# Another tile order in the second dilated attention stage, and the turned blocks beside one step

## The reference

```python
oa, _ = banded_attention(qa, ka, va, WINDOW_A, S, sink)    # 8 heads of 64, keys within 128 tokens
oa = rms_norm(oa.reshape(n, S, D_A), g_oa)
ob = dilated_mixture(qb, kb, vb)                           # 8 heads of 64, each key of the stream by its mask
ob = rms_norm(ob.reshape(n, S, D_B), g_ob)
return jnp.concatenate([oa, ob], axis=-1) @ w_out
```

## Time and profile before

| what | value |
|---|---|
| median of three runs | 2294.83 us (2293.78 to 2295.69) |
| profiled execution: time, span | 2295.82 us, 2294.0 us |
| mean granted TensorE clock | 0.984 |
| TensorE busy | 2194.8 us (96%) |
| VectorE, ScalarE, GpSimd busy | 49%, 28%, 34% |

### The profile page before, as it was taken

The page is one execution under the profiler, slowest core; times in us unless marked ns, Lnnn a source line. Parts: engine busy times, 40 slices in busy tenths (PEclk is TensorE's granted clock), DMA queues, the critical chain, the costliest instruction groups (busy, mean ns, idle before and its releaser), DMA issues. The chain is left out here.

```text
span 2294.0 us, 35862 instructions
## 1 busy us (share of the span) xinstructions
PE 2194.8 (96%) x13528; PEld 1928.1 (84%) x13528; DVE 1134.4 (49%) x2157; ACT 631.9 (28%) x1562; POOL 787.3 (34%) x442
## 2 busy tenths in 40 slices
PE   7999989999999999999998999999999999999997
PEld 7889877888888888888898888789878888888885
DVE  3575655536555145325355766454465532542353
ACT  3445454234311011001044454443242110110002
POOL 3311202441344444444331111034323444444443
PEclk9999989999999999999999999799999999999998
DMA  6200021321122211222241000122111122222222
GB/s 214 71 19 29 29 74 36 93 74 34 51 65 64 64 62 58 64 64 64 65 147 38 29 29 28 65 83 67 62 38 56 57 63 64 64 64 64 64 64 84
DMA packets 41988, 144.86 MB, mean 63 GB/s; under 512 B 4880, under 2 KB 5136, under 8 KB 41616
## 3 DMA queue, kind: packets, MB, share of 16 engines
q1 hardware_dynamic: 34560, 119.02, 16.7%
q10 hardware_dynamic: 7312, 24.21, 3.0%
HBM read 133.78 MB, written 9.44 MB: 62 GB/s over the span
## 5 line engine op out<-in xcount | busy, mean ns | idle before, releaser
L751 POOL CAST w_hi<-w_landed_tile 128x1024 fp32r<-128x1024 f32 x216 | 225.1, 1042 | 1468.7 <-PE ps L798 1456.6
L798 PE MATMUL ps<-x_turned,w_hi 128*128 128x512 f32 (+1 forms) x3072 | 666.7, 339 | 3.6 <-DVE regions L1470 1.9
L798 PEld LDWEIGHTS ps<-x_turned,w_hi 128*128 128x128 f32 x3072 | 523.0, 188 | 106.5 <-issue 5.5
L798 PE MATMUL ps<-w_hi,x_turned 128*128 128x256 f32 (+1 forms) x2304 | 546.9, 320 | 17.3 <-ACT scratch L1224 12.0
L753 POOL TENSOR_TENSOR w_lo<-w_landed_tile,w_hi 128x1024 fp32r<-128x1024 f32 x216 | 554.6, 2567 | 17.3
L798 PEld LDWEIGHTS ps<-w_hi,x_turned 128*128 128x128 f32 x2304 | 390.9, 193 | 42.6 <-issue 9.3
L798 PE MATMUL ps<-x_turned,w_lo 128*128 128x512 f32 (+1 forms) x1536 | 394.3, 338 | 0.0
L798 PE MATMUL ps<-w_hi,regions 128*128 128x512 f32 (+1 forms) x1312 | 374.5, 369 | 0.0
L798 PE MATMUL ps<-w_lo,x_turned 128*128 128x256 f32 (+1 forms) x1152 | 359.6, 312 | 0.0
L798 PEld LDWEIGHTS ps<-w_hi,regions 128*128 128x128 f32 x1312 | 238.7, 188 | 42.0 <-issue 0.7
L1274 ACT ACTIVATE scratch<-scratch 128x768 f32<-128x768 f32 x44 | 37.3, 848 | 839.1 <-DVE scratch L1540 839.1
(11 more groups left out here) (93 smaller groups left out, 2106.6 us busy)
## 6 DMA issues: line engine op xcount, KB each, us to landing
w_landed_tile<-weights_dram SPq DMA_DIRECT2D x216, 512.0 KB, 3.5
x_hbm<-x_residual ACTq DMA_DIRECT2D x2, 3072.0 KB, 14.4
x_residual<-x_hbm ACTq DMA_DIRECT2D x4, 1536.0 KB, 8.4
rows<-mem_in_dram ACTq DMA_DIRECT2D x8, 512.0 KB, 4.5
scratch<-mem_in_dram ACTq DMA_DIRECT2D x8, 512.0 KB, 6.5
x_residual<-x_in_dram SPq DMA_DIRECT2D x12, 256.0 KB, 5.8
gain<-gains_dram ACTq DMA_DIRECT2D x3, 512.0 KB, 15.4
out<-x_residual ACTq DMA_DIRECT2D x6, 256.0 KB, 3.7
```

The source lines that it names most:

```text
L751: nc.gpsimd.tensor_copy(W_HI[:, s, :], W_IN[:, s, :]).then_inc(w_rounded, 1)
L798: ins = pe.matmul(dst, lhsT, rhs, start=start, stop=stop, skip_group_check=True)
```

## The change

The stage B1 takes the tiles in the order 4, 5, 0, 1, 2, 3. A and B0 keep theirs. A group's number is now its place in this order, so waits and squares that know the tile look up the place. The nine entries of the first list all stand beside step 36, and the 38 entries of the second are spread over steps 37 to 49.

```diff
+def tiles_of(stage):
+
+    return (4, 5, 0, 1, 2, 3) if stage == "B1" else tuple(range(NT))
...
-    for t in range(NT):
+    for t in tiles_of(stage):
...
-            step.append(("square", "ob1", full[2]))
+            step.append(("square", "ob1", tiles_of("B1")[full[2]]))
...
-    items += weave(steps[b - 1:b + 2], turned)
-    items += weave(steps[b + 2:], beside)
+    items += weave(steps[b - 1:b], turned)
+    items += weave(steps[b:], beside)
...
-                        group = ("A", 2 * last + 1) if k < 4 else (("B0", "B1")[k // 2 - 2], last)
+                        stage = ("B0", "B1")[k // 2 - 2]
+                        group = ("A", 2 * last + 1) if k < 4 else (stage, tiles_of(stage).index(last))
...
-                            act.wait_ge(normalised, at(l, ("normalise", stage, t)))
+                            act.wait_ge(normalised, at(l, ("normalise", stage, tiles_of(stage).index(t))))
```

## The result

The changed kernel takes 2321.24 us (median of six runs, 2316.43 to 2326.03), the kernel before 2295.26 (six runs beside them). The ratio is 1.0108, 95% interval 1.0094 to 1.0123: **slower by 26 us**, where 8 were forecast.

A forecast was written before the change was run, and what follows sets the result against it. TensorE, busy for 96% of the span, bounds the kernel, so reordering pays only at stops or low clock. Layers +5.3 and +1.0 give +6.3; one fall of 1.7 makes +8.0: forecast 2303 us, range 2299 to 2307.

The forecast's parts named there:

- (b): All eight turned blocks in step 36: steps 36 and 37 take 22.4 us, gaining about 2.2 (layer 0) and 6.6 (layer 1).
- (c): 38 entries over 13 steps: in each layer stops of 2.65 us in steps 41, 43 and 2.1 us in 45, 47.
- (d): Other stops, such as 1.0 and 1.5 us before `t out 4`: 0.5 us better to 1.5 worse in a layer.
- Of four stops of 2.65 and four of 1.0 to 1.5 in narrow steps I count one fall: Clock term for the longer stops of the reordered part: one fall to the low clock, costing 1.7 us.
- the sum without falls: Reordered part at 101.5 us in each layer, +5.3 and +1.0 us, together +6.3.
- none or four: Bounds on the number of added clock falls, each priced at 1.7 us.
- Third rival: Clock falls again and again: four falls, or low past step 38 in one layer; +13.1 up to +17, about 2309; chance 0.18.
- First and second rival: First: stops mostly hidden, about 2298, chance 0.20. Second: clock stays up or returns inside step 36, 2290, chance 0.12.

The follow-up runs named there:

- e3: Changed kernel with eight extra unused products of 512 columns inside each of the four stops of each layer; 2304.66 us.
- e9: e4 with extra unused products in step 36, nine before the first turned block and four before each of the next three, ahead of the bank wait; 2270.44 us.
- e10: e3 with 17 transposes of the identity in place of the eight extra products in each stop; 2303.51 us.
- e7: e3 with four extra products in place of eight ahead of each of the four handoffs; 2316.59 us.
- e1: Changed kernel with the old weave, so only the tile order of the change; 2292.12 us.
- e2: Kernel before with the new weave and the old tile order; 2310.01 us.
- e4: Changed kernel with the 38 entries placed by hand, so no k=3 block is followed in its step by a k=0 block; 2281.75 us.

## Why the prediction was wrong

Wrong was the size: +8 forecast, +26 measured, outside the range that ended at 2311. The direction and the mechanism were right. By its own steps:

- **(b), the turned blocks: right.** 2.68 us from k to k+1 (2.65 predicted), a low stretch of 17.07 us (17), steps 36 and 37 in 319.87 - 297.52 = 22.35 us (22.4).
- **(c), the four stops: right.** The next product came 342.26 - 336.47 = 5.79 us into step 41 (5.85). (The 360.61 taken as the square's end was the start of the work behind it; the square ended at 360.07 + 0.42 = 360.49. `keep` starts as much behind its square, so the sum holds.) Stops of 2.41 and 2.50 on `ACT rows` and of 1.81 and 1.82 on `DVE x_residual` stand in the profile, in the four steps named; with the drain that the prediction counted in, 2.6 and 2.0 (2.65 and 2.1).
- **(d), the rest: right.** No stop on `POOL w_lo` before the first `out`. All but the added falls was put at +6.3; e3, where the clock holds at the handoffs, measured +6.7.
- **"Of four stops of 2.65 and four of 1.0 to 1.5 in narrow steps I count one fall": this term failed**, in two ways. The four stops of 2.65 are those on `keep`, two in each layer; one fall was counted for them, and all four came, of 3.4 us each. The four stops on `add`, 2.1 us each by the prediction's own (c), were left out of the count without a reason; all four brought the clock down too, for 10.2 and 6.8 us in layer 0 and 3.4 and 6.8 us in layer 1, two thirds of the new low time of 41 us. Eight falls and not one: the part takes 112.08 - 101.5 = 10.6 us and 108.67 - 101.5 = 7.2 us more than the sum without falls, 17.8 for the 1.7 of the prediction. e3, which removes the falls and leaves the waits, gave back 16.6.
- The bound given for this term, "none or four", was no bound, since the stops on `add` were not in it. The low stretch at 155.50 behind a stop of 1.51 said that they could count.
- **Third rival**: right in its mechanism, at a chance of 0.18, and too small: it priced four falls at 1.7 us each. What I set against it, that `outa` blocks stand on both sides of the stops, weighed nothing. **First and second rival** fall: the stops were full, and the clock fell where it did before.
- **What the Trainium skill says of transposes** (page TensorE: Matmul & The Clock Gate, Part 4: PE-mode transpose) gave the prediction the right sum for step 36 for the wrong reason. The low clock in step 36 came from the stops between the blocks (e9), not from transposes (e10).

Open: why a fall lasts 3.4 us at one stop and 10.2 at another. In the profiled execution the one at step 45 lasted 10.24 us in layer 0 and 3.42 in layer 1, with the same instructions. Nor does the length of a stop alone decide whether the clock falls. Earlier in layer 0, near 156 us, the changed kernel and those made from it have a stop of 1.51 us, with the same work up to there: in e3 the clock is 0.50 from 156.64 to 160.05 behind it, in e10 it is 1.00 from 155.99 to 159.90.

## What to carry to other kernels

When work is woven between steps, look for pairs in which the second needs what another engine makes of the first, such as the last product into a bank and the first product of the next round: let them meet across a step's end, not within it. Price a stop of TensorE as its length plus a fall of the clock behind it, and count every stop: here eight falls cost some 17 us, beside eight stops of 17 us together (8.5 idle in each layer). Unused products in the stops took the falls away, but not the waits; moving the handoffs took both (39 us). Look also at what a work item wakes on other engines: the first product of a weight tile started a split on POOL, beside which three subtractions of VectorE on the path took 4.90 us instead of 1.90.

## What the runs showed that I had not expected

- The clock fell at stops of 1.81 to 2.51 us in the middle of dense products, eight times in eight. It held there over stops of 1.48 (e7), 1.42 (e1) and 1.19 us (e2). That is no threshold: in the changed kernel it held over a stop of 1.76 us that ended at 38.88, and in the kernel before it fell at 199.87, behind a stop of 1.19 us that ended at 198.18.
- Seventeen float32 transposes back to back in such a stop held the clock as eight products did (2303.5 and 2304.7 us).
- Extra unused products made a kernel faster by 16.6 us (e3) and 11.3 us (e9 against e4).
- Three VectorE subtractions of 512 columns took 4.90 us beside POOL's cast and split, 2.74 with part of them beside it, and 1.90 without it.
